# Output products with norms: casts issued a step ahead, square roots beside their squares, residual sums on GpSimd

## What is computed

```python
# end of a layer of the first block (layers 0 and 1), roughly
h = h + gate * (branches @ w_out)          # the sum is stored and normed
# after layer 1: return rms_norm(h, final_g), which is normed again by the second block
# second block
x = x + mod_x[2] * rms_norm_2(mix_x, mix_post_norm[l])     # mix_x = [attn, ssd] @ w_out
ffn_x = conv_glu(modulate(rms_norm_2(x, ffn_pre_norm[l]), mod_x[3], mod_x[4]), ...)
x = x + mod_x[5] * rms_norm_2(ffn_x, ffn_post_norm[l])
```

## Time and profile before

| | |
|---|---|
| median of 3 runs | 4087.86 us (4080.69 to 4088.53) |
| the profiled execution | 4097.43 us |
| its span, first to last instruction | 4095.6 us |
| PE busy | 3715.4 us, 91% |
| DVE busy | 2601.2 us, 64% |
| ACT busy | 2016.9 us, 49% |
| POOL busy | 974.3 us, 24% |
| mean granted TensorE clock | 0.951 |

### The profile page before, as it was taken

One profiled execution on the slowest core, in us unless ns is written; L12 is line 12 of the kernel. 1 busy time (PEld: TensorE's weight loads), 2 busy tenths in 40 slices (PEclk: granted clock), 3 DMA queues, 4 the chain that ended last, 5 costly groups with the idle time before them and its releaser, 6 DMA issues. The chain is left out here.

```text
span 4095.6 us, 57548 instructions
## 1 busy us (share of the span) xinstructions
PE 3715.4 (91%) x21576; PEld 2913.8 (71%) x21576; DVE 2601.2 (64%) x3871; ACT 2016.9 (49%) x3880; POOL 974.3 (24%) x1080
## 2 busy tenths in 40 slices
PE   6999898888998887888789999999898989999998
PEld 5775677776775676766566666678666768888886
DVE  3766477767765486766555555548966666665655
ACT  4544366645644286644434444455644554444444
POOL 0017103730016004600156555500282000111000
PEclk7989899989989998998899999999999999999999
DMA  5100113445100103351100000022003551111344
GB/s 191 42 16 1 43 46 112 143 138 194 63 21 1 53 21 112 108 186 45 31 5 5 10 6 5 22 94 79 6 9 137 181 159 42 57 47 42 113 149 149
DMA packets 211398, 295.45 MB, mean 72 GB/s; under 512 B 74218, under 2 KB 140010, under 8 KB 211124
## 3 DMA queue, kind: packets, MB, share of 16 engines
q1 hardware_dynamic: 210564, 291.57, 21.4%
q0 software_dynamic: 416, 0.05, 0.0%
q10 hardware_dynamic: 144, 0.15, 0.0%
HBM read 261.12 MB, written 30.51 MB: 71 GB/s over the span
## 5 line engine op out<-in xcount | busy, mean ns | idle before, releaser
L563 DVE TENSOR_TENSOR x_low<-buf_a,x_high 128x640 fp32r<-128x640 f32 (+5 forms) x360 | 357.3, 992 | 305.6 <-ACT x_high L610 288.5
L610 ACT CAST x_high<-buf_a 128x640 fp32r<-128x640 f32 (+5 forms) x360 | 310.9, 864 | 392.7 <-PE ps L670 320.2
L668 PE MATMUL ps<-x_high,w_high 128*128 128x512 f32 (+1 forms) x1184 | 443.9, 375 | 61.5 <-DVE w_low L567 56.0
L669 PE MATMUL ps<-x_low,w_high 128*128 128x512 f32 (+1 forms) x1184 | 437.1, 369 | 0.0
L670 PE MATMUL ps<-x_high,w_low 128*128 128x512 f32 (+1 forms) x1184 | 436.0, 368 | 0.0
L3366 PE MATMUL ps<-w_high,x_high 128*128 128x512 f32 x896 | 363.2, 405 | 65.0 <-DVE w_low L3188 61.2
L3368 PE MATMUL ps<-w_high,x_low 128*128 128x512 f32 x896 | 357.2, 399 | 0.0
L3367 PE MATMUL ps<-w_low,x_high 128*128 128x512 f32 x896 | 356.9, 398 | 0.0
L3948 DVE TENSOR_REDUCE mx<-ps 128x1 fp32r<-128x1280 f32 x128 | 190.7, 1491 | 199.8 <-PE ps L3823 199.3
L3188 DVE TENSOR_TENSOR w_low<-w,w_high 128x1024 fp32r<-128x1024 f32 x170 | 208.0, 1224 | 165.7 <-ACT w_high L3310 165.7
L668 PEld LDWEIGHTS ps<-x_high,w_high 128*128 128x128 f32 x1184 | 226.6, 191 | 109.5 <-DVE x_low L563 64.4
(11 more groups left out here) (450 smaller groups left out, 8884.1 us busy)
## 6 DMA issues: line engine op xcount, KB each, us to landing
w<-in_w_out SPq DMA_DIRECT2D x26, 2048.0 KB, 8.3
w<-in_w_mod SPq DMA_DIRECT2D x24, 2048.0 KB, 9.1
w<-in_w_down SPq DMA_DIRECT2D x15, 2048.0 KB, 7.9
w<-in_w_in SPq DMA_DIRECT2D x26, 1024.0 KB, 5.3
w<-in_w_up SPq DMA_DIRECT2D x22, 1024.0 KB, 7.7
w<-in_w_in SPq DMA_DIRECT2D x6, 2048.0 KB, 8.9
x<-in_x SPq DMA_DIRECT2D x16, 512.0 KB, 8.8
scratch_h<-x SPq DMA_DIRECT2D x8, 512.0 KB
```

The source lines that it names most:

```text
L563: dve.tensor_tensor(part(xl, i)[:, 0:s["tn"]], x_of(s), part(xh, i)[:, 0:s["tn"]].bitcast(F32), ALU.subtract).then_inc(x_low, 1)
L610: act.copy(part(xh, i)[:, 0:s["tn"]], x_of(s)).then_inc(x_high, 1)
L668: pe.matmul(g["out"], lhs[0][:, :], rhs[0][:, :], start=(s["kk"] == 0), stop=False)
L669: pe.matmul(g["out"], lhs[0][:, :], rhs[1][:, :], start=False, stop=False)
```

## The change

1. ScalarE casts a step ahead: at position i it issues the two casts of step i+1 and then the norms of position i (`look_ahead`, `split`). In call D it doesn't, nor does it for position 8 in call C.
2. `mean` is gone. The root follows its squares on ScalarE at once: it waits for the squares and takes scale 1/D and a bias tile holding eps (set once at the start).
3. In calls A, B and C the residual sums are done by GpSimd, in order of the tiles, each as soon as its x and its drained (or gated) product are there. In call D they stay on VectorE.
4. The positions move. ScalarE squares a tile one position ahead of VectorE's scaling; in call A the scaling stands at positions 2, 3, 4, in B and C at 3, 4, 5. The transposes stand at 3, 4, 5 in A and at 4, 5, 6 in B and C. The moves out of PSUM stay at 5, 6, 7. In C and in the tail behind it, ScalarE squares the first product at position 0.

```diff
-        order = [(kind, j) for j in range(3) for kind in ("pre", "main")]
+        order = [("pre", 0), ("pre", 1), ("main", 0), ("pre", 2), ("main", 1), ("main", 2)]
...
+    scale_from = 2 if post is None and pre is None else 3
...
+    def wait_summed(engine, n):
+
+        if n >= nf:
+            engine.wait_ge(summed, n - nf + 1)
+
+    def look_ahead(i):
+
+        alone = lambda n: after is not None or beside is not None and steps[n]["kk"] == KD
+        mine = [i] if i == 0 or alone(i) else []
+        return mine + [n for n in (i + 1,) if n < S and not alone(n)]
...
+                for n in range(nf, nt):
+                    x = xs[n % NS]
+                    pool.wait_ge(x_in[n % NS], 16 * (n // NS + 1))
+                    if post is not None:
+                        pool.wait_ge(gated, n - nf + 1)
+                    else:
+                        wait_drained(pool, n)
+                    pool.tensor_tensor(x[:, :], tmp[(n - nf) % NB][:, :], x[:, :], ALU.add).then_inc(summed, 1)
...
-            def mean(n, kind):
-
-                dve.wait_ge(squared, sq_index[n, kind])
-                st = stat[:, slot_of[kind], :, n]
-                dve.tensor_scalar(st[:, 1:2], st[:, 0:1], 1.0 / D, EPS, ALU.mult, ALU.add).then_inc(chain, 1)
...
+                elif xt is None:
                     if 2 <= kk <= 4:
+                        tile_of(add, mine, kk - 2)
+                    if kk <= 3:
+                        tile_of(norm_after, mine, kk - 1)
+                else:
+                    if pre is not None and 2 <= kk <= 4:
                         tile_of(norm_before, mine, kk - 2)
+                    if post is not None and kk <= 3:
+                        tile_of(norm_after, mine, kk - 1)
+                    if scale_from <= kk < scale_from + 3:
+                        tile_of(scale, mine, kk - scale_from)
                     if kk >= 5:
                         tile_of(transposes_out, mine, kk - 5)
...
                 act.activation(trash[:, :], data, ACT.Square, accum_out=st[:, 0:1]).then_inc(squared, 1)
+                act.wait_ge(squared, sq_index[n, kind])
+                act.activation(st[:, 1:2], st[:, 0:1], ACT.Sqrt, bias=k.eps[:, 0:1], scale=1.0 / D).then_inc(rooted, 1)
...
+                if post is not None and kk <= 2:
+                    tile_of(square_post, mine, kk)
+                if pre is not None and 1 <= kk <= 3:
+                    tile_of(square_pre, mine, kk - 1)
+                if scale_from - 1 <= kk < scale_from + 2:
+                    tile_of(square_main, mine, kk - scale_from + 1)
+                if kk >= 5:
+                    tile_of(transposes_out, mine, kk - 5)
...
+            for i, s in enumerate(steps):
+                for n in look_ahead(i):
+                    split(n)
                 if ahead and i == 0:
                     ahead.act(act)
                 norms(s["pos"], before[s["g"]])
...
-            turn_at = (4, 5, 6) if pre is not None else (3, 4, 6)
+            turn_at = (4, 5, 6) if scale_from == 3 else (3, 4, 5)
...
+                    elif tiles[n]["res"]:
+                        wait_summed(sp, n)
                     sp.dma_start(tiles[n]["store"], xs[n % NS][:, :]).then_inc(stored[n % NS], 16)
```

More of the change, by code:

```diff
@@ L3002, in project_normalize @@
         assert post is None
-        order = [(kind, j) for j in range(3) for kind in ("pre", "main")]
+        order = [("pre", 0), ("pre", 1), ("main", 0), ("pre", 2), ("main", 1), ("main", 2)]
     else:
-        order = [("post", 0), ("main", 0), ("post", 1), ("main", 1), ("post", 2), ("main", 2)]
+        order = [(kind, j) for kind in ("post", "main") for j in range(3)]
     sq_index, i = {}, 0
@@ L3098, in drain @@
                 b = tmp[(n - nf) % NB]
+                if xt is not None:
+                    wait_summed(dve, n - NB)
                 if post is None:
@@ L3115, in add @@
             def add(n):
-                w, x = tiles[n], xs[n % NS]
+                x = xs[n % NS]
                 dve.wait_ge(x_in[n % NS], 16 * (n // NS + 1))
[L3118 to L3124, removed]
+                dve.wait_ge(gated, n - nf + 1)
+                dve.tensor_tensor(x[:, :], tmp[(n - nf) % NB][:, :], x[:, :], ALU.add).then_inc(summed, 1)
             def norm_before(n):
@@ L3135, in scale @@
             def scale(n):
-                mean(n, "main")
                 if n >= 2:
@@ L3231, in drain @@
                     act.wait_ge(ws.products, product_of[n])
-                    if n - NB >= nf:
-                        act.wait_ge(chain, step_ready[n - NB, "sum"])
+                    wait_summed(act, n - NB)
                     act.copy(tmp[(n - nf) % NB][:, :], y_of(n)).then_inc(drained_act, 1)
@@ L3239, in square_post @@
                     square_root(n, "post", tmp[(n - nf) % NB][:, :])
-                    root(n, "post")
             def square_pre(n):
                 if tiles[n]["res"]:
-                    act.wait_ge(chain, step_ready[n, "sum"])
+                    wait_summed(act, n)
                     square_root(n, "pre", xs[n % NS][:, :])
             def square_main(n):
-                if tiles[n]["res"]:
-                    act.wait_ge(chain, step_ready[n, "sum2" if pre is not None else "sum"])
+                if tiles[n]["res"] and pre is not None:
+                    act.wait_ge(chain, step_ready[n, "sum2"])
+                elif tiles[n]["res"]:
+                    wait_summed(act, n)
                 else:
@@ L3252, in square_main @@
                 square_root(n, "main", xs[n % NS][:, :])
-            def root_main(n):
-                root(n, "main")
-            def root_pre(n):
-                if tiles[n]["res"]:
-                    root(n, "pre")
             def norms(kk, mine):
@@ L4422, in first, with _ @@
 def first(k):
-    (in_,) = sems = k.sems("identity_in")
+    (in_, set_) = sems = k.sems("identity_in", "eps_set")
     with k.stage() as block:
+        @block.vector
+        def _(dve):
+            dve.memset(k.eps[:, :], EPS).then_inc(set_, 1)
+            dve.wait_ge(set_, 1)
         @block.sync
@@ L4438, in build_program @@
         k.ident = k.at("ident", [P, P], A_C)
+        k.eps = k.at("eps", [P, 1], A_C + 704)
         k.ws = WeightStream(k, *weight_plan(d))
```

78 lines of the change are left out of this document (7 added, 71 removed).

## The result

The changed kernel takes 4107.2 us (median of 7 runs, 4101.2 to 4112.5) against 4088.5 for the kernel before (7 runs on the same chip, 4077.4 to 4096.7): a ratio of 1.005, 95% interval 1.0034 to 1.0066. It is slower by about half a per cent; the forecast was 4086 with a range to 4104. Its profiled execution took 4101.17 us, the span 4099.3.

A forecast was written before the change was run, and what follows sets the result against it. It saw latency, chiefly ScalarE and VectorE handing tiles to and fro in B, then two-tile groups. B +21, A -11.8, C -9.9, D +2.3 gave 1.6 us gained: 4087.9 to 4086, range 4064 to 4104.

The forecast's parts named there:

- Turn and drain stalls: TensorE waits for ScalarE behind casts: five of 2.75 us in A, five of 2.35 and two of 2.3 in C.
- B: Call B gains 21 us: groups 1, 7.3 and 9.7, waits behind it 3.
- the root's hand-over: ScalarE and VectorE hand one tile to and fro in B; ScalarE's root waits 1.36 us for `mean`.
- the walk: Step-by-step timing of B's last group with the change: end at 31.4 us, not 41.1, 9.7 gained.
- Sums: GpSimd adds in A, B, C block VectorE subtractions 2.4 us unless under a drain; blocks counted 24.7 us in all.
- a rival with 0.27 at 4100: New gaps in A and C lower TensorE's granted clock there; steps cost 14 us more; 4100, chance 0.27.
- The argument against the clock: A's third group ran at clock 1.00 with a fifth of its time lost, so gaps need not lower it.
- D: Call D's last group loses a `mean` and a wait in three steps, about 0.8 at the end; gain 2.3 us.
- A 11.8 forecast: Call A loses 11.8 us: second group 6.6, third 3.2, fourth 1.5, tail 0.5.
- C 9.9: Call C loses 9.9 us: StateNorm's stalls 11.8 lost, three-tile group 0.9 and tail 1 gained.

The follow-up runs named there:

- e3: Changed kernel with ScalarE's drains and moves out of PSUM issued before the next step's cast, squares and roots still behind it; 4070.8 us, ratio 0.9953 to the kernel before.
- e9: Kernel before with only the joined roots: root right behind its squares on ScalarE, VectorE's means gone; 4079.5 us, ratio 0.9973 to the kernel before.
- e10: Kernel before with only the sums of A, B and C moved to GpSimd; 4096.2 us, ratio 1.0019 to the kernel before.
- e4: Changed kernel with the 26 sums back on VectorE, all else kept; 4080.2 us, ratio 0.9983 to the kernel before.
- e12: Changed kernel with products of zeros filling TensorE's stalls at StateNorm's turns in C's first two groups; 4099.3 us, ratio 1.0025 to the kernel before.

## Why the prediction was wrong

The forecast was a gain of 1.6 us, and the calls lost 14.8. The clock and the late weights, taken at nothing, are some 15 of these 16.4 us.

- **Turn and drain stalls: right.** Ten turn stalls at 2.2 to 2.8 us and two drain stalls at 2.2, in the places named. The releaser that was argued from the queues is the one that e3 removed.
- **B: right in size (21 forecast, 23.1 measured), less so in its reason.** The second group gained 8.1 (7.3 forecast), the last 9.4 (9.7), the tail 4.1 (3). But I put the root's hand-over first; alone it gives 3.9 us (e9). And some of the gain is clock, which the walk did not count: the granted clock of these two groups was 0.96 and 0.88 before and is 1.00 and 0.95 after.
- **Sums: right in size, in part by luck.** 24.7 us were counted as the cost of the blocks; undoing them gives 27 by the ratio and 19.3 by the calls. But low clock behind the blocked steps, which was not counted, is part of this price. The Trainium skill (SBUF — State Buffer, Who interferes with whom) states that a VectorE instruction with two SBUF inputs contends with a GpSimd instruction that reads SBUF. The trace agrees, with subtractions of 3.40 and 2.75 us. What the rule leaves open, and e10 shows, is that the same 26 sums cost 8 us in one order and 27 in another.
- **The clock: the step that failed.** The sum took full clock in A and C and left a lower grant to a rival with 0.27 at 4100. Steps of products became longer, each against the same step at full clock: in A 1.7 (second group, position 6), 1.3 (third, position 1) and 2.5 (last, position 1), 5.5 us in all; in C 1.5, 1.6 and 1.6 (first, positions 6, 12, 14), 1.6 (second, position 13), 1.6 and 1.3 (last, positions 0 and 4), 9.2 in all. The kernel before had two such steps in C, of 1.6 and about 1.7 us (second group, position 4, and last, position 3), and none in these groups of A. So the clock cost 5.5 us more in A and about 5.9 in C.
- **What these steps stood behind.** 8.0 of the 14.7 us come behind the turn and drain stalls. The other waits are for the low weight part. 5.1 us (1.3, 2.5 and 1.3) come behind waits of 3.0, 3.1 and 3.0 us. The first two of these shrink when the sums go back to VectorE (e4), and the low clock with them. And 1.6 come behind the late weights. The rival had thought of the ten turn stalls alone; its price of 14 us (15, if 174 us are divided by 0.92) was near what came.
- **The argument against the clock** was that A's third group ran at 1.00 with a fifth of its time lost. It compared total lost time; in that group the gaps in front of TensorE's steps were 0.5 to 1.5 us each, and the new ones are 1.8 to 3.1. The Trainium skill (TensorE: Matmul & The Clock Gate, Part 1) says that the clock is gated by how busy the array has been. e12 agrees: filled stalls, 0.71 back to 1.00.
- **SyncE in C: the step that was left out.** The squares of StateNorm were moved, and SyncE's z tiles wait for them with the weight load queued behind. It cost 3.8 us in the changed kernel (8.66 instead of 4.88 for position 11), besides the 1.6 of low clock at position 12. The working followed every instruction of the moved part on ScalarE and VectorE, and no DMA that waits for one.
- **D: right** (2.3 forecast, 2.7 measured).

By call: A 11.8 forecast and 18.7 measured, of the 6.9 between them the clock 5.5; C 9.9 and 22.0, of the 12.1 between them the clock about 5.9 and the weights 3.8. The medians differ by 18.7 us and the calls by 14.8. The rest lies in stretches that the change doesn't touch, which differ between executions by more than that (the first product of A started at 882.5 us in the profile of before and between 871.9 and 880.9 in the others); whether the 4 us are chance stays open. With the 14.8 us of the calls alone the time would have been 4103.3, just inside the range, so it is these 4 us, and no part of the argument, that put it 3 us above.

## What to carry to other kernels

When work is moved to a later step, list whoever waits for it on every queue, the DMA issuer first: what is queued behind that waiter moves too. Looking ahead with a cast is good for the cast and bad for whatever is issued behind it, so put what another engine waits for (drains, moves out of PSUM) ahead of the cast that itself waits, and the rest behind. Price the stalls of TensorE with what they may do to the clock of the next steps, whoever makes TensorE wait: here 8.0 us behind 29 us of turn and drain stalls, and 5.1 more behind three waits for VectorE. And price a shared port in the new order, not in the old: the same 26 sums cost 8 us in one and 27 in the other.

## What the runs showed of the hardware

In the changed kernel TensorE's granted clock fell to its lower level, 1.2 GHz, for part or all of a step behind two stalls of 2.2 to 2.8 us one step apart, behind single ones of 2.19 and 2.39 us, and behind single waits of 3.0 to 3.5 us. It did not fall each time. Behind the pair of 2.69 us stalls in A's third group the next step took 2.84 us, at full clock. Behind the stall of 2.19 us in front of C's second group the step took 4.27 us in the changed kernel and 5.81 in e12, and behind a wait of 1.83 us in A it took 4.20 and 5.81. Behind the pair of stalls in C's first group it fell each time in the changed kernel and in e4, and with the stalls filled by products of zeros (2.20 us for nine), which computed nothing, it stayed at 2.4 GHz (one profile, two steps). A 128x1024 VectorE subtraction beside back-to-back GpSimd sums took 3.40 us instead of 1.23, and a 128x384 one 2.75 instead of 0.55.
